# The gated convolution's input projection with its three column blocks walked innermost, in two sets of three PSUM banks

## The chip, the cores and the metric

One core of a Trainium2 chip runs the whole program. The metric is the device time of one execution in microseconds (us), the median over several runs. PSUM is the accumulator memory that TensorE writes; it has eight banks here, and one matmul writes into one bank.

## The reference, cut to what matters

The program is one inference step of a small decoder: a gated short convolution layer, shared keys and values, one forgetting-attention layer, and a gated feed after each of the two layers. It runs on 1024 prompt tokens and 64 sample tokens, 1088 columns in all. The change lies in the convolution layer, in the product `h @ w_in`:

```python
def short_conv_layer(x, conv_state, g, w_in, conv_w, w_out):
    h = rmsnorm(x, g)
    b_gate, c_gate, xin, z = jnp.split(h @ w_in, 4, axis=-1)
    u = c_gate * xin
    u_pad = jnp.concatenate([conv_state.astype(u.dtype), u], axis=1)
    T = u.shape[1]
    conv = conv_w[0] * u_pad[:, 0:T]
    for j in range(1, CONV_W):
        conv = conv + conv_w[j] * u_pad[:, j:j + T]
    y = b_gate * conv * jax.nn.silu(z)
    return x + y @ w_out, u_pad[:, -(CONV_W - 1):]
```

`h` has 1024 features, `w_in` is 1024 x 4096, everything is float32.

## The kernel before

Activations lie transposed: 128 features on the partitions, the 1088 tokens along the free axis, eight such chunks k = 0 to 7 (`KC`). The tokens are cut into three column blocks (`BLK`): 364, 364 and 360 columns. An fp32 product is made of three cheaper ones: each operand is split into a rounded part and a rest (`w_hi` and `w_lo`, `Hhi` and `Hlo`), and `w_hi*Hhi`, `w_hi*Hlo` and `w_lo*Hhi` are added up in PSUM (lines 560, 561, 562). An output tile is 128 output features by 1088 tokens: 3 blocks x 8 chunks x 3 products = 72 matmuls, each with a weight load of its own.

The input projection is 32 such tiles: a loop over j = 0 to 7, and in it t = 0 to 3 for the four parts of `w_in` (c_gate, xin, z, b_gate in that order). Line 615 calls `tile(...)` with bank 0, so that every tile writes banks 0, 1 and 2, one for each column block. `tile` has two orders:

- With `hr` given (t = 0 here) chunk k is the outer loop, since at the start of the stage the chunks of h arrive one by one: for each k it makes three products of block 0, three of block 1, three of block 2. The bank changes after each three products.
- Without `hr` (t = 1, 2, 3) the block is the outer loop: all 24 products of block 0, then those of block 1, then those of block 2. The bank changes after 24 products.

Before the first product of a block, `free(b)` makes TensorE wait until the bank's last content has been taken out; the last product of a block raises the semaphore `block_done`. What takes a tile out of PSUM differs: t = 0 is copied to scrA by ScalarE (line 984), t = 1 is multiplied with scrA into scrU by VectorE (lines 1293 and 1295), t = 2 goes through ScalarE's silu into scrZ (line 986), t = 3 is multiplied with scrC into Y by VectorE (line 1319). These raise `act_evac` (ScalarE) and `dve_evac` (VectorE), three per tile.

Beside that, the same engines prepare weights. The weight buffers are doubled (`par`): SyncE loads tile n's weights, GpSimd multiplies in the norm's gain (line 490), ScalarE makes `w_hi` (line 937) as soon as tile n - 2 is done with the buffer, VectorE makes `w_lo` (line 1232), and that releases TensorE (`w_split`). Each engine's queue is in order: on VectorE `w_lo` of tile j, t = 3 stands behind the convolution of t = 1 (lines 1299 to 1311), and on ScalarE `w_hi` for the next tile stands behind the three evacuations of t = 0 or t = 2.

After the 32 tiles comes the output projection, whose operand Y is split in two by ScalarE and VectorE (lines 967 and 1261); it may begin when all of Y is written. Its tiles, and those of the feed, go through the same `tile` function with `hr` given for every other tile.

Of the kernel before, what the change touches and what calls it, by code (L numbers as in the profile page):

```python
# [20 lines left out]
ALU = mybir.AluOpType  # L21
# [45 lines left out]
for _kb in range(8):  # L67
# [11 lines left out]
    "tensor": {"block_done": 6, "score": 1, "turned": 1, "pv": 1, "s_score": 2, "s_pv": 1},  # L79
    "vector": {"n0_acc": 2, "n1_acc": 2, "n2_acc": 2, "w_split": 2, "x_sum": 2, "dve_evac": 6, "o_free": 1, "o_done": 1,  # L80
               "p_lo": 1, "s_kt1": 1, "s_pt1": 1, "s_osb": 1, "s_out": 1},
    "scalar": {"exp": 1, "s_kt0": 1, "s_exp": 1, "s_pt0": 1},
    "sync": {"kv_out": 16, "y_out": 16},
}
START = {name: n for per in LEAD.values() for name, n in per.items()}
# [7 lines left out]
def program(nc, a, o, d):  # L93

    es = ExitStack()
    with es:
# [451 lines left out]
        def _(pe):  # L548
            for k, n in LEAD["tensor"].items():
                pe.sem_inc(sems[k], n)  # L550
            mm, tp = pe.matmul, pe.transpose

            def tile(n, par, bank, free, hr=None, k0=0, nk=KC, hi=Hhi, lo=Hlo):

                pe.wait_ge(sems["w_split"], START["w_split"] + n + 1)
                def products(b, k):
                    s, e = BLK[b]
                    out = PS[:, bank + b, 0:e - s]
                    wh, wl = whi[:, par, k0 + k, :], wlo[:, par, k0 + k, :]
                    mm(out, wh, hi[:, k, s:e], start=(k == 0), stop=False)  # L560
                    mm(out, wh, lo[:, k, s:e], start=False, stop=False)  # L561
                    last = mm(out, wl, hi[:, k, s:e], start=False, stop=(k == nk - 1))  # L562
                    if k == nk - 1:
                        last.then_inc(sems["block_done"], 1)
                if hr is not None:
                    for k in range(nk):
                        pe.wait_ge(sems["h_ready"], hr + k + 1)
                        for b in range(NB):
                            if k == 0:
                                free(b)  # L570
                            products(b, k)
                else:
                    for b in range(NB):
                        free(b)
                        for k in range(nk):
                            products(b, k)
# [33 lines left out]
            with pe.Fori(0, KC) as j:  # L610
                for t in range(4):

                    free = [lambda b: pe.wait_ge(sems["dve_evac"], START["dve_evac"] + 6 * j - 3 + b + 1), lambda b: pe.wait_ge(sems["act_evac"], 6 * j + b + 1),
                            lambda b: pe.wait_ge(sems["dve_evac"], START["dve_evac"] + 6 * j + b + 1), lambda b: pe.wait_ge(sems["act_evac"], 6 * j + 3 + b + 1)][t]
                    tile(4 * j + t, t % 2, 0, free, hr=0 if t == 0 else None)

            def out_tiles(n0, ed0, hr):
                with pe.Fori(0, KC // 2) as i:
# [4 lines left out]
            def feed(r, n0, ea0, ed0, hr):  # L623

                pe.wait_ge(sems[f"ple{r}_in"], 48)
                for c in range(PC):
                    for h_, src in enumerate((sA, sZ, sU)):
                        if c:
                            pe.wait_ge(sems[f"ple{r}_lo"], h_ + 1)
                        if h_ < 2:  # L630
                            for i in range(4):
                                last = tp(PS[:, 3 + h_, i * P:(i + 1) * P], src[:, i * PLE + c * P:i * PLE + (c + 1) * P], ident[:, :])
                        else:
                            last = tp(PS[:, 5, 0:NS], src[0:NS, c * P:(c + 1) * P], ident[0:NS, 0:NS])
                        last.then_inc(sems[f"ple{r}_turned"], 1)
                pe.wait_ge(sems[f"ple{r}_lo"], 6)
                pe.wait_ge(sems["dve_evac"], START["dve_evac"] + ed0)
                with pe.Fori(0, KC // 2) as i:
                    for u in range(2):
                        n, par = n0 + 2 * i + u, (n0 + u) % 2  # L640
                        tile(n, par, 0, lambda b: pe.wait_ge(sems["act_evac"], ea0 + 6 * i + 3 * u - 3 + b + 1), hr=hr if u == 0 else None)
                        tile(n, par, 3, lambda b: pe.wait_ge(sems["dve_evac"], START["dve_evac"] + ed0 + 6 * i + 3 * u - 3 + b + 1),
                             k0=KC, nk=PC, hi=PTh, lo=PTl)

# [5 lines left out]
            feed(0, N_A3, EA_A3, ED_A3, 16)  # L650
            norm_sum(1)

            pe.wait_ge(sems["act_evac"], EA_F)
            tile(N_F, N_F % 2, 0, lambda b: None, hr=24)

            pe.wait_ge(sems["s_logf"], 16 * DB * PAGES)
# [15 lines left out]
            def dense_piece(j, half, p):  # L672

                i, b, k = 2 * half + p // 24, p % 24 // KC, p % KC
                g_ = 4 * j + 3 + i
                par = (N_B1 + 3 + i) % 2
                if p % 24 == 0:
                    pe.wait_ge(sems["w_split"], START["w_split"] + N_B1 + g_ + 1)
                if k == 0:
                    pe.wait_ge(sems["act_evac"], EA_B1 + 3 * g_ - 3 + b + 1)  # L680
                s, e = BLK[b]
                out = PS[:, b, 0:e - s]
                wh, wl = whi[:, par, k, :], wlo[:, par, k, :]
                mm(out, wh, Hhi[:, k, s:e], start=(k == 0), stop=False)  # L684
                mm(out, wh, Hlo[:, k, s:e], start=False, stop=False)  # L685
                last = mm(out, wl, Hhi[:, k, s:e], start=False, stop=(k == KC - 1))  # L686
                if k == KC - 1:
                    last.then_inc(sems["block_done"], 1)
# [87 lines left out]
            half_pair(NPAIR - 1, 1, False)  # L776


            pe.wait_ge(sems["act_evac"], EA_B2)
            pe.wait_ge(sems["exp"], START["exp"] + 16 * NPAIR)  # L780
            pe.wait_ge(sems["p_lo"], START["p_lo"] + 24 * NPAIR)
            pe.wait_ge(sems["o_done"], START["o_done"] + 4 * NPAIR)
# [121 lines left out]
            out_tiles(N_B2, ED_B2, 32)  # L904
            feed(1, N_B3, EA_B3, ED_B3, 40)
            pe.wait_ge(sems["dve_evac"], START["dve_evac"] + ED_END)
            pe.wait_ge(sems["act_evac"], EA_END)
            pe.wait_ge(sems["n2_acc"], START["n2_acc"] + KC)
            for tt in range(9):
                n = P if tt < 8 else NS  # L910
# [313 lines left out]
        def _(ve):  # L1224
# [56 lines left out]
            def conv_layer(j, last):  # L1281
                for t in range(4):
# [4 lines left out]
                    ve.drain()  # L1287
                    if t == 1:
                        for b, (s, e) in enumerate(BLK):
                            ve.wait_ge(sems["act_evac"], 6 * j + b + 1)  # L1290
                            ve.wait_ge(sems["block_done"], START["block_done"] + 12 * j + 3 + b + 1)
                            m = min(e, SEQ)
                            ins = tt_(Up[:, 2 + s:2 + m], PS[:, b, 0:m - s], sA[:, s:m], ALU.mult)
                            if e > SEQ:
                                ins = tt_(Us[:, :, 2:], PS[:, b, SEQ - s:e - s].rearrange("p (b t) -> p b t", b=DB),
                                          sA[:, SEQ:e].rearrange("p (b t) -> p b t", b=DB), ALU.mult)
                            ins.then_inc(sems["dve_evac"], 1)
                        g = lambda r, n=1: GT[:, bass.ds(j, 1), r:r + n].rearrange("p a n -> p (a n)")
                        ve.tensor_copy(Us[:, :, 0:2], g(G_ST, 16).rearrange("p (b w) -> p b w", b=DB))
                        ve.drain()  # L1300
                        cs = sC[:, SEQ:].rearrange("p (b t) -> p b t", b=DB)
                        for w in range(CW):
                            for dst, src in ((sC[:, 0:SEQ], Up[:, w:w + SEQ]), (cs, Us[:, :, w:w + DS])):
                                if w == 0:
                                    ts_(dst, src, g(G_CW), None, ALU.mult)
                                else:
                                    stt(out=dst, in0=src, scalar=g(G_CW + w), in1=dst, op0=ALU.mult, op1=ALU.add)
                            ve.drain()
                        ucj = at_pair(uc, j).rearrange("p a n -> p (a n)")
                        ve.tensor_copy(ucj[:, 0:2], Up[:, SEQ:SEQ + 2])  # L1310
                        ve.tensor_copy(ucj[:, 2:18].rearrange("p (b w) -> p b w", b=DB), Us[:, :, DS:])
                    if t == 2:
                        ve.wait_ge(sems["act_evac"], 6 * j + 6)
                        tt_(sC[:, :], sC[:, :], sZ[:, :], ALU.mult)
                        ve.drain()
                    if t == 3:
                        for b, (s, e) in enumerate(BLK):
                            ve.wait_ge(sems["block_done"], START["block_done"] + 12 * j + 9 + b + 1)
                            tt_(at_pair(Y, j).rearrange("p a n -> p (a n)")[:, s:e], PS[:, b, 0:e - s], sC[:, s:e],
                                ALU.mult).then_inc(sems["dve_evac"], 1)  # L1320
            peeled(ve, KC, conv_layer)

# [20 lines left out]
            def feed(r, n0, b0, ea0, h0):  # L1343
# [10 lines left out]
                def body(i, last):  # L1354
                    for u in range(2):
# [4 lines left out]
                        else:  # L1360
                            w_lo(n % 2, n + 2 * i, nk=KC + PC)
                        for b, (s, e) in enumerate(BLK):
                            ve.wait_ge(sems["act_evac"], ea0 + 6 * i + 3 * u + b + 1)
                            ve.wait_ge(sems["block_done"], START["block_done"] + b0 + 12 * i + 6 * u + 3 + b + 1)
                            tt_(sg[:, u, s:e], sg[:, u, s:e], PS[:, 3 + b, 0:e - s], ALU.mult).then_inc(sems["dve_evac"], 1)
                        ve.drain()
# [291 lines left out]
```

## Time and profile before

| | us |
|---|---|
| median of 3 runs (lowest, highest) | 1946.63 (1946.03, 1947.12) |
| profiled execution, first to last instruction (its span) | 1943.1 |
| TensorE busy with matmuls | 1765.1 |
| VectorE busy | 885.6 |
| ScalarE busy | 721.3 |
| GpSimd busy | 265.3 |

The profiled execution has no other time of its own than its span; the median of the runs is 3.5 us more, which is what lies around the first and last instruction. A matmul's recorded duration includes its way through the array and is a model; two matmuls in a row overlap in the rows. What a matmul costs in a stream is the distance from its start to the next one's start. Starts are printed to 0.01 us. The granted clock of TensorE is printed as a share of full speed; 1.00 is 2.4 GHz and 0.50 is 1.2 GHz.

### The profile page before, as it was taken

How to read it: one execution, taken by the hardware profiler on the slowest of the kernel's cores; microseconds unless marked ns; L12 is line 12 of the kernel's file. 1: busy time of each engine (PE TensorE's matmuls, PEld its weight loads, DVE VectorE, ACT ScalarE, POOL GpSimd, SP SyncE). 2: the span in 40 equal slices, each digit the busy share in tenths (PEclk: the TensorE clock that was granted, in tenths of full speed). 3: DMA queues.
4: the chain of work that ended last, by engine and by line, in shares of the span. 5: the costliest groups of instructions: out<-in, count | busy, mean ns of one | idle time of the engine just before them, and what ended most of it. 6: DMA issues, size and time to landing. Idle time of an engine off the chain costs nothing.

```text
span 1943.1 us, 33338 instructions
## 1 busy us (share of the span) xinstructions
PE 1765.1 (91%) x11871; PEld 1611.6 (83%) x11871; DVE 885.6 (46%) x1379; ACT 721.3 (37%) x1174; POOL 265.3 (14%) x229
## 2 busy tenths in 40 slices
PE   3699999999999958999999999999779999899997
PEld 2699999999989948888888888888656666699997
DVE  5722222224253374555555556555544444523543
ACT  3311211112043233565656555565533233401432
POOL 1311111110000021222222122222110000000010
PEclk7999999999999979999999999999869999899998
DMA  3011111111211023211101021110318778721102
GB/s 127 23 45 45 47 50 47 45 44 44 72 41 42 8 97 92 57 46 34 56 23 59 19 78 45 34 56 23 132 51 307 265 269 327 276 86 57 41 27 92
DMA packets 163424, 161.57 MB, mean 83 GB/s; under 512 B 18188, under 2 KB 140172, under 8 KB 163126
## 3 DMA queue, kind: packets, MB, share of 16 engines
q1 hardware_dynamic: 163382, 161.03, 24.9%
q8 instruction: 24, 0.39, 0.1%
q14 instruction: 18, 0.15, 0.0%
HBM read 137.20 MB, written 23.80 MB: 83 GB/s over the span
## 4 chain that ended last, share of the span: by engine, by line
PE 73%; DVE 10%; ACT 6%; issue 5%; DVEq 3%; ACTq 2%; POOL 1%; DMA 0%; SPq 0%; POOLq 0%
PE PS L560 14%; PE PS L562 14%; PE PS L561 14%; PE PS L684 4%; PE PS L686 3%; PE PS L685 3%; PE PS L743 3%; PE PS L790 3%; PE PS L731 2%; DVE small L1410 2%; PE PS L857 2%; PE PS L714 2%; PE PS L812 2%; DVE pTl L1421 1%; DVE Hlo L1261 1%
## 5 line engine op out<-in xcount | busy, mean ns | idle before, releaser
L560 PE MATMUL PS<-Hhi,w_hi 128*128 128x364 f32 (+1 forms) x1560 | 519.3, 333 | 58.7 <-DVE Hlo L1261 57.6
L562 PE MATMUL PS<-Hhi,w_lo 128*128 128x364 f32 (+1 forms) x1560 | 515.8, 331 | 0.0
L561 PE MATMUL PS<-Hlo,w_hi 128*128 128x364 f32 (+1 forms) x1560 | 513.4, 329 | 0.0
L560 PEld LDWEIGHTS PS<-Hhi,w_hi 128*128 128x128 f32 x1560 | 297.2, 190 | 66.2 <-issue 44.2
L561 PEld LDWEIGHTS PS<-Hlo,w_hi 128*128 128x128 f32 x1560 | 296.6, 190 | 0.0
L562 PEld LDWEIGHTS PS<-Hhi,w_lo 128*128 128x128 f32 x1560 | 296.1, 190 | 0.0
L684 PE MATMUL PS<-Hhi,w_hi 128*128 128x364 f32 (+1 forms) x768 | 274.0, 357 | 0.1
L686 PE MATMUL PS<-Hhi,w_lo 128*128 128x364 f32 (+1 forms) x768 | 252.4, 329 | 0.0
L685 PE MATMUL PS<-Hlo,w_hi 128*128 128x364 f32 (+1 forms) x768 | 251.8, 328 | 0.0
L490 POOL TENSOR_TENSOR w_raw<-w_raw,GT 128x1024 f32<-128x1024 f32 x65 | 128.6, 1980 | 692.8 <-DMA w_raw<-in_w_kv 383.2
L937 ACT ACTIVATE w_hi<-w_raw 128x1024 fp32r<-128x1024 f32 (+1 forms) x97 | 105.8, 1091 | 293.4 <-PE PS L562 289.4
L1232 DVE TENSOR_TENSOR w_lo<-w_raw,w_hi 128x1024 fp32r<-128x1024 f32 (+1 forms) x97 | 126.0, 1299 | 140.2 <-ACT w_hi L937 136.7
L1421 DVE TENSOR_TENSOR pTl<-PS,pTh 128x512 fp32r<-128x512 f32 x192 | 103.5, 554 | 122.6 <-ACT pTh L1067 120.2
L1059 ACT ACTIVATE Pb<-PS,small 128x128 f32<-128x128 f32 (+7 forms) x128 | 94.8, 740 | 160.8 <-DVE small L1410 160.8
L684 PEld LDWEIGHTS PS<-Hhi,w_hi 128*128 128x128 f32 x768 | 146.8, 191 | 0.7 <-DVE w_lo L1232 0.2
L519 POOL TENSOR_SCALAR Pb<-Pb,small 128x128 f32<-128x128 f32 (+7 forms) x128 | 95.1, 747 | 378.1 <-DVE small L1415 378.1
L685 PEld LDWEIGHTS PS<-Hlo,w_hi 128*128 128x128 f32 x768 | 145.9, 190 | 0.0
L686 PEld LDWEIGHTS PS<-Hhi,w_lo 128*128 128x128 f32 x768 | 144.7, 188 | 0.0
L1067 ACT ACTIVATE pTh<-PS 128x512 fp32r<-128x512 f32 x192 | 89.7, 487 | 96.9 <-PE PS L731 93.6
L1410 DVE TENSOR_REDUCE small<-PS 128x1 f32<-128x128 f32 (+7 forms) x128 | 95.6, 748 | 37.2 <-PE PS L717 36.9
L743 PE MATMUL PS<-pTh,VS 128*128 128x512 f32 x192 | 73.5, 383 | 35.1 <-DVE pTl L1421 35.0
L731 PE MATMUL PS<-ident,Pb 128*128 128x128 f32 x576 | 94.5, 285 | 6.7 <-POOL Pb L519 6.7
(230 smaller groups left out, 2286.3 us busy)
## 6 DMA issues: line engine op xcount, KB each, us to landing
Kpages<-in_cache_k SPq DMA_DIRECT2D x64, 512.0 KB, 5.7
Vpages<-in_cache_v SPq DMA_DIRECT2D x64, 512.0 KB, 5.5
w_raw<-in_w_in_a SPq DMA_DIRECT2D x64, 256.0 KB, 3.0
w_raw<-in_w_ple_gate SPq DMA_DIRECT2D x16, 512.0 KB, 3.7
w_raw<-in_w_kv SPq DMA_DIRECT2D x32, 256.0 KB, 3.1
w_raw<-in_w_in_b SPq DMA_DIRECT2D x32, 256.0 KB, 3.0
parked_x<-X SPq DMA_DIRECT2D x8, 544.0 KB, 5.0
X<-parked_x SPq DMA_DIRECT2D x8, 544.0 KB, 7.7
```

Source lines behind the costliest of these rows:

```text
L490: g.tensor_tensor(w, w, GT[:, :, r:r + 1].to_broadcast([P, KC, P]), ALU.mult).then_inc(sems["w_gained"], 1)
L560: mm(out, wh, hi[:, k, s:e], start=(k == 0), stop=False)
L561: mm(out, wh, lo[:, k, s:e], start=False, stop=False)
L562: last = mm(out, wl, hi[:, k, s:e], start=False, stop=(k == nk - 1))
L684: mm(out, wh, Hhi[:, k, s:e], start=(k == 0), stop=False)
L685: mm(out, wh, Hlo[:, k, s:e], start=False, stop=False)
L686: last = mm(out, wl, Hhi[:, k, s:e], start=False, stop=(k == KC - 1))
L731: last = tp(PS[:, 5 + kb % 2, qi * P:(qi + 1) * P], Pb[:, off:off + P], ident[:, :])
L743: last = mm(PS[:, 7, q0 * P:512], VS[:, kb, hh, :], x[:, kb % 2, q0 * P:512], start=(kb == 0 and x is pTh), stop=(kb == nkb - 1 and x is pTl))
L1232: tt_(wlo[:, par, 0:nk, :], raw[:, par, 0:nk, :], f(whi[:, par, 0:nk, :]), ALU.subtract).then_inc(sems["w_split"], 1)
L1410: ve.reduce_max(small[:, qb:qb + 1], score_bank(qb)[:, 0:n], AXX, negate=True).then_inc(sems["rowmax"], 1)
L1421: tt_(pTl[:, kb % 2, q0 * P:512], PS[:, 5 + kb % 2, q0 * P:512], f(pTh[:, kb % 2, q0 * P:512]), ALU.subtract).then_inc(sems["p_lo"], 1)
```

## The change

A new function `across` replaces `tile` for the 32 tiles of the input projection. Chunk k stays or becomes the outer loop, in it come the three products, and the three column blocks are innermost. So the first product of a chunk is made for blocks 0, 1 and 2, then the second, then the third, and each matmul writes another bank than the one before. The three sums of a tile are open at the same time and all end with the tile's last three matmuls. Tiles alternate between banks 0 to 2 (t = 0 and 2) and banks 3 to 5 (t = 1 and 3); before a tile's first product one wait asks for the last block of the tile two before it to be taken out. To make that wait hold in the first round, `act_evac` starts at 6, and every wait on it adds that offset.

```diff
-    "scalar": {"exp": 1, "s_kt0": 1, "s_exp": 1, "s_pt0": 1},
+    "scalar": {"act_evac": 6, "exp": 1, "s_kt0": 1, "s_exp": 1, "s_pt0": 1},
...
+            def across(n, par, bank, free, hr=None):
+
+                pe.wait_ge(sems["w_split"], START["w_split"] + n + 1)
+                free(NB - 1)
+                for k in range(KC):
+                    if hr is not None:
+                        pe.wait_ge(sems["h_ready"], hr + k + 1)
+                    wh, wl = whi[:, par, k, :], wlo[:, par, k, :]
+                    for x, (w, h) in enumerate(((wh, Hhi), (wh, Hlo), (wl, Hhi))):
+                        for b, (s, e) in enumerate(BLK):
+                            last = mm(PS[:, bank + b, 0:e - s], w, h[:, k, s:e], start=(k == 0 and x == 0), stop=(k == KC - 1 and x == 2))
+                            if k == KC - 1 and x == 2:
+                                last.then_inc(sems["block_done"], 1)
...
-                    free = [lambda b: pe.wait_ge(sems["dve_evac"], START["dve_evac"] + 6 * j - 3 + b + 1), lambda b: pe.wait_ge(sems["act_evac"], 6 * j + b + 1),
-                            lambda b: pe.wait_ge(sems["dve_evac"], START["dve_evac"] + 6 * j + b + 1), lambda b: pe.wait_ge(sems["act_evac"], 6 * j + 3 + b + 1)][t]
-                    tile(4 * j + t, t % 2, 0, free, hr=0 if t == 0 else None)
+                    free = [lambda b: pe.wait_ge(sems["act_evac"], START["act_evac"] + 6 * j - 3 + b + 1), lambda b: pe.wait_ge(sems["dve_evac"], START["dve_evac"] + 6 * j - 3 + b + 1),
+                            lambda b: pe.wait_ge(sems["act_evac"], START["act_evac"] + 6 * j + b + 1), lambda b: pe.wait_ge(sems["dve_evac"], START["dve_evac"] + 6 * j + b + 1)][t]
+                    across(4 * j + t, t % 2, 3 * (t % 2), free, hr=0 if t == 0 else None)
...
-                            ins = tt_(Up[:, 2 + s:2 + m], PS[:, b, 0:m - s], sA[:, s:m], ALU.mult)
+                            ins = tt_(Up[:, 2 + s:2 + m], PS[:, 3 + b, 0:m - s], sA[:, s:m], ALU.mult)
...
-                            tt_(at_pair(Y, j).rearrange("p a n -> p (a n)")[:, s:e], PS[:, b, 0:e - s], sC[:, s:e],
+                            tt_(at_pair(Y, j).rearrange("p a n -> p (a n)")[:, s:e], PS[:, 3 + b, 0:e - s], sC[:, s:e],
```

The rest of the diff adds `START["act_evac"]` to the other waits on `act_evac`.

## Rows read from the trace of the kernel before

**Rows 1.** The page's head: the span, and the busy time of each engine.

```profile
span 1943.1 us, 33338 instructions
...
PE 1765.1 (91%) x11871; PEld 1611.6 (83%) x11871; DVE 885.6 (46%) x1379; ACT 721.3 (37%) x1174; POOL 265.3 (14%) x229
```

**Rows 2.** Busy time by window, tiles 2 to 31: window, length, each engine's busy, PEclk, DMA.

```profile
90.81:448.90 358.09, 358.08 (x2162) 357.53 (x2160) 105.53 (x163) 69.81 (x88) 51.78 (x27) 1.00 0.16 45
```

**Rows 3.** Timeline of TensorE (start, duration): first products of tiles and blocks.

```profile
78.80 0.43 PE L560 MATMUL PS<-Hhi,w_hi 128*128 128x364 f32 x1 [1.19 <-DVE w_lo L1232]
...
162.43 0.33 PE L560 MATMUL PS<-Hhi,w_hi 128*128 128x364 f32 x1
...
174.29 0.33 PE L560 MATMUL PS<-Hhi,w_hi 128*128 128x364 f32 x1
...
178.29 0.33 PE L560 MATMUL PS<-Hhi,w_hi 128*128 128x364 f32 x1
...
182.25 0.32 PE L560 MATMUL PS<-Hhi,w_hi 128*128 128x360 f32 x1
...
186.24 0.33 PE L560 MATMUL PS<-Hhi,w_hi 128*128 128x364 f32 x1
```

**Rows 4.** Timeline of TensorE, one chunk of a t = 0 tile: bank changes.

```profile
122.13 0.33 PE L560 MATMUL PS<-Hhi,w_hi 128*128 128x364 f32 x1
...
122.46 0.33 PE L562 MATMUL PS<-Hhi,w_lo 128*128 128x364 f32 x1
122.63 0.33 PE L560 MATMUL PS<-Hhi,w_hi 128*128 128x364 f32 x1
...
122.96 0.33 PE L562 MATMUL PS<-Hhi,w_lo 128*128 128x364 f32 x1
123.12 0.33 PE L560 MATMUL PS<-Hhi,w_hi 128*128 128x360 f32 x1
...
123.45 0.32 PE L562 MATMUL PS<-Hhi,w_lo 128*128 128x360 f32 x1
123.61 0.33 PE L560 MATMUL PS<-Hhi,w_hi 128*128 128x364 f32 x1
```

**Rows 5.** Feed after the output projection, at half clock: two timeline rows, one window.

```profile
557.23 0.50 PE L560 MATMUL PS<-Hhi,w_hi 128*128 128x360 f32 x1
...
558.13 0.51 PE L560 MATMUL PS<-Hhi,w_hi 128*128 128x364 f32 x1
...
555.20:559.70 4.50, 4.45 (x15) 4.46 (x16) 4.50 (x4) 4.50 (x6) 0.00 (x0) 0.50 0.00 0
```

**Rows 6.** Timeline of VectorE after tile t = 1: last evacuation, next two weight splits.

```profile
138.72 0.47 DVE L1293 TENSOR_TENSOR scrU<-PS,scrA 128x296 f32<-128x296 f32 x1 [3.45 <-PE PS L562]
...
144.20 1.23 DVE L1232 TENSOR_TENSOR w_lo<-w_raw,w_hi 128x1024 fp32r<-128x1024 f32 x1
...
152.67 1.23 DVE L1232 TENSOR_TENSOR w_lo<-w_raw,w_hi 128x1024 fp32r<-128x1024 f32 x1
```

**Rows 7.** Timeline of ScalarE: evacuation of a t = 0 tile, and a weight split.

```profile
125.79 1.45 ACT L984 ACTIVATE scrA<-PS 128x364 f32<-128x364 f32 x3 [9.80 <-PE PS L562]
...
151.35 1.07 ACT L937 ACTIVATE w_hi<-w_raw 128x1024 fp32r<-128x1024 f32 x1 [0.20 <-issue]
```

**Rows 8.** Timeline, all engines: the end of the stage.

```profile
448.93 0.53 DVE L1319 TENSOR_TENSOR Y<-PS,scrC 128x360 f32<-128x360 f32 x1 [3.45 <-PE PS L562]
449.49 4.12 ACT L967 ACTIVATE Hhi<-Y 128x1088 fp32r<-128x1088 f32 x4 [10.85 <-DVE Y L1319]
...
452.17 0.43 PE L560 MATMUL PS<-Hhi,w_hi 128*128 128x364 f32 x1 [3.28 <-DVE Hlo L1261]
```

**Rows 9.** Windows after idle TensorE: the clock behind two such gaps.

```profile
452.20:464.00 11.80, 11.80 (x72) 11.77 (x72) 9.84 (x10) 6.36 (x7) 0.00 (x0) 1.00 0.10 27
...
1675.80:1679.20 3.40, 0.07 (x1) 0.07 (x2) 2.88 (x5) 1.54 (x5) 0.00 (x0) 1.00 1.03 414
1679.30:1682.70 3.40, 3.40 (x17) 3.16 (x17) 0.97 (x3) 2.55 (x6) 0.00 (x0) 0.50 0.65 266
```

More of the change, by code:

```diff
@@ L640, in feed @@
                         n, par = n0 + 2 * i + u, (n0 + u) % 2
-                        tile(n, par, 0, lambda b: pe.wait_ge(sems["act_evac"], ea0 + 6 * i + 3 * u - 3 + b + 1), hr=hr if u == 0 else None)
+                        tile(n, par, 0, lambda b: pe.wait_ge(sems["act_evac"], START["act_evac"] + ea0 + 6 * i + 3 * u - 3 + b + 1), hr=hr if u == 0 else None)
                         tile(n, par, 3, lambda b: pe.wait_ge(sems["dve_evac"], START["dve_evac"] + ed0 + 6 * i + 3 * u - 3 + b + 1),
@@ L651, in _ @@
             norm_sum(1)
-            pe.wait_ge(sems["act_evac"], EA_F)
+            pe.wait_ge(sems["act_evac"], START["act_evac"] + EA_F)
             tile(N_F, N_F % 2, 0, lambda b: None, hr=24)
@@ L679, in dense_piece @@
                 if k == 0:
-                    pe.wait_ge(sems["act_evac"], EA_B1 + 3 * g_ - 3 + b + 1)
+                    pe.wait_ge(sems["act_evac"], START["act_evac"] + EA_B1 + 3 * g_ - 3 + b + 1)
                 s, e = BLK[b]
@@ L776, in _ @@
             half_pair(NPAIR - 1, 1, False)
-            pe.wait_ge(sems["act_evac"], EA_B2)
+            pe.wait_ge(sems["act_evac"], START["act_evac"] + EA_B2)
             pe.wait_ge(sems["exp"], START["exp"] + 16 * NPAIR)
@@ L906, in _ @@
             pe.wait_ge(sems["dve_evac"], START["dve_evac"] + ED_END)
-            pe.wait_ge(sems["act_evac"], EA_END)
+            pe.wait_ge(sems["act_evac"], START["act_evac"] + EA_END)
             pe.wait_ge(sems["n2_acc"], START["n2_acc"] + KC)
@@ L1289, in conv_layer @@
                         for b, (s, e) in enumerate(BLK):
-                            ve.wait_ge(sems["act_evac"], 6 * j + b + 1)
+                            ve.wait_ge(sems["act_evac"], START["act_evac"] + 6 * j + b + 1)
                             ve.wait_ge(sems["block_done"], START["block_done"] + 12 * j + 3 + b + 1)
                             m = min(e, SEQ)
-                            ins = tt_(Up[:, 2 + s:2 + m], PS[:, b, 0:m - s], sA[:, s:m], ALU.mult)
+                            ins = tt_(Up[:, 2 + s:2 + m], PS[:, 3 + b, 0:m - s], sA[:, s:m], ALU.mult)
                             if e > SEQ:
-                                ins = tt_(Us[:, :, 2:], PS[:, b, SEQ - s:e - s].rearrange("p (b t) -> p b t", b=DB),
+                                ins = tt_(Us[:, :, 2:], PS[:, 3 + b, SEQ - s:e - s].rearrange("p (b t) -> p b t", b=DB),
                                           sA[:, SEQ:e].rearrange("p (b t) -> p b t", b=DB), ALU.mult)
@@ L1312, in conv_layer @@
                     if t == 2:
-                        ve.wait_ge(sems["act_evac"], 6 * j + 6)
+                        ve.wait_ge(sems["act_evac"], START["act_evac"] + 6 * j + 6)
                         tt_(sC[:, :], sC[:, :], sZ[:, :], ALU.mult)
@@ L1362, in body @@
                         for b, (s, e) in enumerate(BLK):
-                            ve.wait_ge(sems["act_evac"], ea0 + 6 * i + 3 * u + b + 1)
+                            ve.wait_ge(sems["act_evac"], START["act_evac"] + ea0 + 6 * i + 3 * u + b + 1)
                             ve.wait_ge(sems["block_done"], START["block_done"] + b0 + 12 * i + 6 * u + 3 + b + 1)
```

## The prediction, made before the change was run

> **What bounds the kernel now.** I read the page's head first: of a span of 1943.1 us TensorE is busy 91%, VectorE 46%, ScalarE 37% [rows 1]. The span is 3.5 us under the median of the runs, 1946.63; I take those 3.5 us as fixed and make the sum against 1946.63. Then the windows over the stage that changes: from the start of tile 2 to the end of tile 31 TensorE is busy for 358.08 of 358.09 us, at the full clock, while VectorE has work for 105.53 and ScalarE for 69.81 us [rows 2]. So nothing waits in this stage; only a shorter distance between products, or a new wait, can move its time.
>
> Then the timeline of TensorE, for that distance. A t = 0 tile, bank changing after three products, lasts 174.29 - 162.43 = 11.86 us; the t = 1 tile behind it, bank changing after 24, 186.24 - 174.29 = 11.95 us [rows 3]. That is 11.86/72 = 164.7 ns and 11.95/72 = 166.0 ns a product. Over the stage (8 tiles of the first kind, 24 of the second) the mean is 165.7 ns for 2304 products. This pair is a small trial of the change that the trace already holds: same data and same number of products, other order.
>
> What is in those 166 ns? In the half-clock window behind the stage three products of 360 columns take 558.13 - 557.23 = 0.90 us, 300 ns each [rows 5], which is 360 columns at 1.2 GHz and nothing else. At 2.4 GHz the mean of 362.7 columns would then be 151.1 ns; the stage has 14.6 ns more. A cost of writing the same bank again, if it were counted in TensorE's own cycles, would show at half clock as well, where the three products also share a bank. It doesn't.
>
> **The change part by part.**
>
> Order of products in t = 1, 2, 3. The number of products and of weight loads stays. Now the bank changes with every product; the trace has no row for that. Nearest is the t = 0 tile. In one of its chunks the step is 123.61 - 122.13 = 1.48 us for nine products (164.4 ns), and the distances across a change of bank read 0.17 (bank 0 to 1), 0.16 (1 to 2) and 0.16 (2 to 0) [rows 4]. In the block-wise tile the first block takes 4.00 us for 24 products, the second 3.96, the third 3.99 although its products are four columns shorter [rows 3]: the distance follows the pattern of lengths and starts more than the bank. I take the t = 0 tile's value for all tiles: 24 x (11.86 - 11.95) = -2.2 us. Both bounds come from the printed starts, which show 0.16 or 0.17: at 160 ns 2304 x -5.7 = -13.1 us, at 170 ns 2304 x 4.3 = +9.9 us. The value is nearer the middle because each of the three changes of bank that the new order repeats stands in rows 4, and 0.49 us over three is 163 ns, with up to 0.01 us of rounding in each.
>
> Order in t = 0: it changes only from three in a row to one; at the same value it costs nothing. In tile 0 each chunk still waits for h, in the same order.
>
> Evacuations. Until now a block-wise tile's first two blocks were taken out beside its own products; now all three end together and are taken out beside the next tile. With t = 0 that is so already: three copies, 1.45 us in all from 125.79, around that tile's end at 162.43 - 3 x 11.95 = 126.58, and no gap on TensorE [rows 2, 3, 7]. For t = 1, VectorE's two earlier multiplies move behind the tile's end, some 2 x 0.5 us. Behind them stand the convolution and `w_lo` for t = 3, which now ends at 144.20 + 1.23 = 145.43 us [rows 6]; at 146.4 it would still be about 4 us ahead of tile t = 3, which begins one tile length before the next t = 0 tile, at 162.43 - 11.95 = 150.48 [rows 3]. For t = 2, two silu evacuations (0.5 us each, as the copies) move behind the tile's end, ahead of `w_hi` at 151.35 and `w_lo` at 152.67 [rows 6, 7]; 1 us later than 153.9 is still over 7 us ahead of 162.43. The PSUM waits ask for the tile two before, a whole tile (11.9 us) back, and its evacuation ends 2 us after it. So these moves cost nothing, covered by the next tile's products; without that cover each would add up to 1 us a tile, 32 us in all. The wait of tile 1 for its first weights, 1.19 us [rows 3], is set by weight preparation ahead of any evacuation and stays.
>
> The Trainium skill speaks against the change here: its page Perfetto Trace Analysis (Optimizing Tensor Performance, Matmuls) wants independent groups to rotate through banks so that one group's evacuation runs beside the next one's products. By that rule, read strictly for the three groups of a tile, those 32 us would be lost; by rows 3 and 7 the second set of banks keeps the cover, except in the last tile.
>
> The last tile has no cover. Its last multiply began at 448.93, the split of Y followed at 449.49 and TensorE began again at 452.17 [rows 8]. Now three multiplies begin about two products earlier (448.6) and take some 0.5 us each, so Y is whole at about 450.1 instead of 449.46: +0.7 us. Weight prefetch is not late: its DMAs and gains wait for the weight splits, which move by under 1 us.
>
> Offsets: one semaphore increment at ScalarE's start, long before its first work, and two PSUM waits fewer per tile. Nothing, as no gap stands at a tile's start now [rows 2].
>
> Clock at that gap. TensorE idles 3.28 us there now, and the clock stays at 1.00 afterwards [rows 8, 9]; elsewhere 3.40 us of near idleness were followed by 3.40 us at 0.50 [rows 9]. With 4 us idle a drop is possible. It would cost half of its length, so 1.7 us for 3.4 and 3.4 us for twice that. I leave it out of the sum (the gap stays short) and put it in the range.
>
> Sum: -2.2 + 0.7 = -1.5 us, 1945.1 us. A measurement of this kernel can tell 0.2%, 3.9 us, from no change; so this counts as no change.
>
> **The rivals.**
>
> The gain grows with the changes of bank. A t = 0 tile has 24 changes, the others 3; 0.09 us over 21 is 4.3 ns each. With 72 in every tile: 24 x 69 x 4.3 ns = 7.1 us and 8 x 48 x 4.3 ns = 1.7 us, so -8.8 + 0.7: 1938.5 us. For it: the t = 0 tile is the shorter one [rows 3]. Against it: the distances across a change [rows 4] are not shorter than those within a bank as a whole.
>
> Same-bank accumulation is the whole excess. 2304 x 14.6 ns = 33.6 us, so 1913.7 us. Rows 4 and 5 speak against it. The Trainium skill's page TensorE: Matmul & The Clock Gate (Back-to-back issue gap) gives columns/2.4 GHz + 2.5 ns for a lone stream, 153.6 ns here, an estimate by which about 28 us could be won; the same section says that with weight loads both set the spacing, and the trace has a load for each product and 165.7 ns, so it bears out the second statement.
>
> The order lands in the long pattern (slower). Place: every product of the 32 tiles. Its price is that of the change from bank 0 to bank 1, 0.17 us [rows 4]; if all three changes took that, 2304 x 4.3 = +9.9, with the +0.7 at the end 1957.2 us. It decides from 165.7 + (3.9 - 0.7)/2304 = 167.1 ns a product. Against it: the other two changes read 0.16.
>
> Nothing changes in the products: each tile keeps its distance and only the end is paid, 1947.3 us. That is also the case in which the order isn't what sets the 14.6 ns at all.
>
> **How the numbers follow.** Forecast 1945.1 us: 0.46. Gain by bank change: 0.26. Whole excess: 0.04. Long pattern: 0.12. Nothing in the products: 0.12. So faster 0.30, same 0.46 + 0.12 = 0.58, slower 0.12. The forecast's own range is 1943 to 1948.5 (with a clock drop of 3.4 us). The range leaves out the whole excess and the long pattern and goes from 1937.0, just under the gain by bank change, to 1949.5, the case of nothing in the products with most of a clock drop.
>
> **What would show it.** Right: tiles of about 11.86 us for every t, TensorE without gaps from tile 2 to 31, the three last multiplies in a row and TensorE back 0.7 us later after them. A step of nine products at 1.44 us or less would be the gain by bank change, at 1.51 or more the long pattern. Wrong altogether: an idle row ahead of a tile's first product, named by `w_lo`, scrA or scrZ, or fewer weight loads than products.

## The result: slower by 0.16%, and the profile after

| | before | changed |
|---|---|---|
| median of 15 runs each (us) | 1946.63 | 1950.62 |
| lowest, highest | 1945.05, 1951.39 | 1945.21, 1952.16 |
| span of the profiled execution | 1943.1 | 1948.5 |

The ratio of the changed kernel to the one before is 1.0016, 95% interval 1.0009 to 1.0024, so 1.8 to 4.7 us are lost. A second comparison gave 1.0018 (1.0009 to 1.0028). The forecast was 1945.1 us, with a range up to 1949.5. Four executions in the comparisons of this study took over 500 us longer than the others of their kernel, and the ratios and the spreads below leave them out. The changed kernel's profiled execution took 1950.32 us, 1.8 us more than its span of 1948.5. All 15 executions lie 1.7 to 1.8 us above their own spans, so only about half of the 3.5 us that I had read as lying around the span does so; the rest would be the spread between executions.

The head of the page after, beside [rows 1]: the same number of matmuls, and TensorE busy for 6.1 us more, where the span is 5.4 us longer. So the longer span is time in which TensorE works, not time in which it waits.

```profile
span 1948.5 us, 33291 instructions
...
PE 1771.2 (91%) x11871; PEld 1616.8 (83%) x11871; DVE 882.6 (45%) x1379; ACT 718.2 (37%) x1174; POOL 265.2 (14%) x229
```

The window of [rows 2] again, in the changed kernel. No new wait: TensorE is busy throughout, but in the same time it makes 2151 products instead of 2162. (The counts in brackets take in products that reach into the window.)

```profile
90.81:448.90 358.09, 358.09 (x2151) 358.09 (x2150) 102.37 (x163) 66.56 (x88) 51.73 (x27) 1.00 0.16 45
```

Timeline of TensorE in the changed kernel, the answer to [rows 3, 4]. The first three rows are first products of three tiles in a row (t = 0, 1, 2); the other three stand for three products each, one in each bank.

```profile
163.50 0.33 PE L563 MATMUL PS<-Hhi,w_hi 128*128 128x364 f32 x1
...
175.50 0.33 PE L563 MATMUL PS<-Hhi,w_hi 128*128 128x364 f32 x1
...
187.50 0.33 PE L563 MATMUL PS<-Hhi,w_hi 128*128 128x364 f32 x1
...
450.00 0.66 PE L563 MATMUL PS<-Hhi,w_hi 128*128 128x364 f32 x3
450.50 0.66 PE L563 MATMUL PS<-Hlo,w_hi 128*128 128x364 f32 x3
451.00 0.66 PE L563 MATMUL PS<-Hhi,w_lo 128*128 128x364 f32 x3
```

From tile 2 on every tile takes 12.00 us, where it was 11.86 or 11.95. The step is 0.50 us for three products, 166.7 ns each, and it stays that regular to the last tile. (Tile 0 waits for the chunks of h; tile 1, which starts after the wait for its weights, takes 12.09 us.) The end of the stage, all engines, and the clock behind it, beside [rows 8, 9]:

```profile
451.36 1.42 DVE L1333 TENSOR_TENSOR Y<-PS,scrC 128x364 f32<-128x364 f32 x3 [8.11 <-PE PS L563]
452.81 1.11 ACT L981 ACTIVATE Hhi<-Y 128x1088 fp32r<-128x1088 f32 x1 [10.99 <-DVE Y L1333]
...
455.49 0.67 PE L574 MATMUL PS<-Hhi,w_hi 128*128 128x364 f32 x1 [3.83 <-DVE Hlo L1275]
...
455.40:458.90 3.50, 3.41 (x11) 3.42 (x12) 3.50 (x4) 3.50 (x5) 0.00 (x0) 0.51 0.00 0
```

The three multiplies now stand in one row, all behind the tile's end, and TensorE's gap is 3.83 us instead of 3.28. Behind it the clock is at half speed for 3.4 us, which it wasn't before.

Against the profile before, the differences of matching products give the account. The first product of tile 1 comes 0.60 us later (78.80 to 79.40); it waits for its weights there as before, and two profiles of the unchanged kernel differ at that point by 0.56 us, so I don't count this to the change. The last product of the stage is 2.77 us later, so the products cost 2.17. The first output tile begins 3.32 us later: the gap costs 0.55. The second output tile begins 4.88 us later: the half clock costs 1.56. After that the difference stays between 4.86 and 5.06 us up to the last matmul.

### The profile page after: what moved, and what is told of

It reads as the page before. It is cut to its first block, busy times and chain, and to the rows that moved or that the text cites. A ratio compares the mean times of both kernels' runs of the same rounds, so it can differ in the third digit from the quotient of the medians.

```text
span 1948.5 us, 33291 instructions
## 1 busy us (share of the span) xinstructions
PE 1771.2 (91%) x11871; PEld 1616.8 (83%) x11871; DVE 882.6 (45%) x1379; ACT 718.2 (37%) x1174; POOL 265.2 (14%) x229
## 4 chain that ended last, share of the span: by engine, by line
PE 72%; DVE 10%; ACT 6%; issue 5%; DVEq 3%; ACTq 2%; DMA 1%; POOL 1%; SPq 0%; POOLq 0%
PE PS L563 19%; PE PS L574 8%; PE PS L576 7%; PE PS L575 7%; PE PS L698 4%; PE PS L700 3%; PE PS L699 3%; PE PS L757 3%; PE PS L804 3%; PE PS L745 2%; DVE small L1424 2%; PE PS L871 2%; PE PS L728 2%; PE PS L826 2%; DVE pTl L1435 1%
## 5 line engine op out<-in xcount | busy, mean ns | idle before, releaser
L574 PE MATMUL PS<-Hhi,w_hi 128*128 128x364 f32 (+1 forms) x792 | 266.3, 336 | 36.0 <-DVE Hlo L1275 36.0
L698 PE MATMUL PS<-Hhi,w_hi 128*128 128x364 f32 (+1 forms) x768 | 274.0, 357 | 0.1
L576 PE MATMUL PS<-Hhi,w_lo 128*128 128x364 f32 (+1 forms) x792 | 263.0, 332 | 0.0
L575 PE MATMUL PS<-Hlo,w_hi 128*128 128x364 f32 (+1 forms) x792 | 262.6, 332 | 0.0
L700 PE MATMUL PS<-Hhi,w_lo 128*128 128x364 f32 (+1 forms) x768 | 252.4, 329 | 0.0
L699 PE MATMUL PS<-Hlo,w_hi 128*128 128x364 f32 (+1 forms) x768 | 251.9, 328 | 0.0
L563 PE MATMUL PS<-Hhi,w_hi 128*128 128x364 f32 (+1 forms) x768 | 171.3, 331 | 22.7 <-DVE Hlo L1275 21.6
L574 PEld LDWEIGHTS PS<-Hhi,w_hi 128*128 128x128 f32 x792 | 152.5, 193 | 40.1 <-issue 29.7
L563 PE MATMUL PS<-Hlo,w_hi 128*128 128x364 f32 (+1 forms) x768 | 170.5, 330 | 0.0
L563 PE MATMUL PS<-Hhi,w_lo 128*128 128x364 f32 (+1 forms) x768 | 170.1, 330 | 0.0
L563 PEld LDWEIGHTS PS<-Hhi,w_hi 128*128 128x128 f32 x768 | 133.7, 189 | 25.8 <-issue 15.0
L575 PEld LDWEIGHTS PS<-Hlo,w_hi 128*128 128x128 f32 x792 | 152.5, 192 | 0.0
L576 PEld LDWEIGHTS PS<-Hhi,w_lo 128*128 128x128 f32 x792 | 152.0, 192 | 0.0
L698 PEld LDWEIGHTS PS<-Hhi,w_hi 128*128 128x128 f32 x768 | 146.8, 191 | 0.7 <-DVE w_lo L1246 0.2
L699 PEld LDWEIGHTS PS<-Hlo,w_hi 128*128 128x128 f32 x768 | 145.9, 190 | 0.0
L700 PEld LDWEIGHTS PS<-Hhi,w_lo 128*128 128x128 f32 x768 | 144.7, 188 | 0.0
```

The costliest lines, as they stand in the source:

```text
L563: last = mm(PS[:, bank + b, 0:e - s], w, h[:, k, s:e], start=(k == 0 and x == 0), stop=(k == KC - 1 and x == 2))
```

## The experiments

Three things had to be told apart: whether the 12.00 us come from the changes of bank or from the order of operands (which weights and columns follow each other); whether the value belongs to the order at all or can fall either way; and whether the fall of the clock belongs to the longer gap.

**Chunk order in all tiles, two bank sets.** The bank changes at every third product.

```diff
-                    for x, (w, h) in enumerate(((wh, Hhi), (wh, Hlo), (wl, Hhi))):
-                        for b, (s, e) in enumerate(BLK):
+                    for b, (s, e) in enumerate(BLK):
+                        for x, (w, h) in enumerate(((wh, Hhi), (wh, Hlo), (wl, Hhi))):
```

> The changed kernel, but inside a chunk three products of block 0, then three of block 1, then three of block 2 (the bank changes every third product), for all 32 tiles; two bank sets and evacuation at the tile's end stay. Theory A (the distance between products is set by the order of operands, lengths and starts, not by the bank): every tile takes 11.84 to 11.87 us, against 12.00 in the changed kernel and 11.95 in three quarters of the tiles before; the stage is about 2.2 us shorter than before and 4.5 us shorter than in the changed kernel; the gap behind the stage is between 3.3 and 3.8 us. Median 1944 to 1946 us. Theory B (fewer changes of bank are better, since the change with 72 per tile got longer): the tiles lie between 11.95 (3 changes) and 12.00 (72 changes), about 11.97.

Measured: median 1945.08 us, ratio to before 0.9982 (0.9973 to 0.9991). First products of two tiles in a row in its timeline:

```profile
161.68 0.33 PE L563 MATMUL PS<-Hhi,w_hi 128*128 128x364 f32 x1
...
173.52 0.33 PE L563 MATMUL PS<-Hhi,w_hi 128*128 128x364 f32 x1
```

11.84 us for every tile from tile 2 on, the value of theory A and outside that of theory B. Bank sets and evacuations are those of the changed kernel here, so neither of them makes the 12.00 us; the order of the nine products in a chunk does. All 11 executions lie between 1942.43 and 1946.25 us, while 13 of the changed kernel's 15 took 1949.66 us or more. The kernel is faster than before though its clock, too, fell behind the stage, with a gap no longer than before.

**One bank, and banks that rotate.** These two put the changed kernel's order on one bank, and the old order on changing banks. In both, a tile is taken out after its last product; the edits to the evacuations are left out here.

```diff
-                            last = mm(PS[:, bank + b, 0:e - s], w, h[:, k, s:e], start=(k == 0 and x == 0), stop=(k == KC - 1 and x == 2))
+                            last = mm(PS[:, bank, 0:e - s], w, h[:, k, s:e], start=(k == 0 and x == 0 and b == 0), stop=(k == KC - 1 and x == 2 and b == 2))
...
```

> The changed kernel's order of operands to the letter, but all three blocks of a tile are added up in one bank, so the bank never changes within a tile; each tile is taken out after its last product. Its sums leave the three blocks unseparated. Theory A (order of operands): tiles stay at 12.00 us. Theory B (change of bank costs 0.65 ns per product): tiles go back to 11.95 us or under. Theory C (writing the same bank again costs something that the other patterns hide): tiles become longer than 12.00 us, by up to 14 ns per product, 13 us per tile.

```diff
+                m = 0
+                for b, (s, e) in enumerate(BLK):
+                    for k in range(KC):
...
+                            last = mm(PS[:, bank + m % 3, 0:e - s], w, h[:, k, s:e], start=(m < 3), stop=(m >= 69))
+                            m += 1
...
```

> The order of operands of the kernel before (all 24 products of a block, then the next block) in all tiles, but product m writes bank m modulo 3, so the bank changes with every product as in the changed kernel. Its sums are spread over three banks instead of one per block. Theory A (order of operands): tiles of 11.95 us with blocks of 4.00, 3.96 and 3.99 us, as before. Theory B (change of bank): tiles of 12.00 us. Theory C: shorter than 11.95.

Measured, first the kernel with rotating banks and the old order (first products of three tiles in a row):

```profile
169.96 0.33 PE L564 MATMUL PS<-Hhi,w_hi 128*128 128x364 f32 x1
...
181.91 0.33 PE L564 MATMUL PS<-Hhi,w_hi 128*128 128x364 f32 x1
...
193.87 0.33 PE L564 MATMUL PS<-Hhi,w_hi 128*128 128x364 f32 x1
```

11.95 us, with the bank changing at every product: as before, as theory A has it. (Its first tile, block by block too, waits longer for h; its total of 1958.18 us isn't compared.) The other kernel, one bank and the changed order, showed 11.84 us per tile and 1945.75 us. That fits neither theory A (12.00) nor C (longer; its 14 ns a product would be 1 us a tile, not 13); it would fit B, but B wants 12.00 us of the rotating banks, which showed 11.95. So I ran it again with many executions, beside the changed kernel and the kernel before.

> The kernel with the changed kernel's order of operands and one bank per tile once more, now with many executions; its sums leave the three blocks unseparated. Open is whether its 11.84 us per tile belongs to it, or is one of two spacings (1.480 or 1.500 us for nine products) into which the stream of the changed kernel's order may settle in any execution. Theory D (each order and bank pattern has its own spacing): tiles of 11.84 us again, executions in one group about 5 us under those of the changed kernel, near the kernel before. Theory E (drawn anew in each execution, whatever the banks): two groups 5 us apart, some at the level of the changed kernel, and perhaps tiles of 12.00 us in the profile.

> The changed kernel as it is, for another look. Theory D: tiles of 12.00 us again. Theory E: 12.00 or 11.84. In both, the gap behind the stage is 3.8 us; whether the clock falls in it is seen here a second time (it fell in the first profile, and at gaps of 3.4 to 3.6 us in two of the experiments).

Timeline of the one-bank kernel, first run; each row is three products:

```profile
441.08 0.66 PE L563 MATMUL PS<-Hhi,w_hi 128*128 128x364 f32 x3
441.58 0.66 PE L563 MATMUL PS<-Hlo,w_hi 128*128 128x364 f32 x3
442.07 0.66 PE L563 MATMUL PS<-Hhi,w_lo 128*128 128x364 f32 x3
442.56 0.49 PE L563 MATMUL PS<-Hhi,w_hi 128*128 128x364 f32 x2
```

And the same kernel, second run:

```profile
440.38 0.66 PE L563 MATMUL PS<-Hhi,w_hi 128*128 128x364 f32 x3
440.88 0.66 PE L563 MATMUL PS<-Hlo,w_hi 128*128 128x364 f32 x3
441.38 0.66 PE L563 MATMUL PS<-Hhi,w_lo 128*128 128x364 f32 x3
441.88 0.66 PE L563 MATMUL PS<-Hhi,w_hi 128*128 128x364 f32 x3
```

1.48 us for nine products in one run, 1.50 in the other: the same instructions, two spacings, each held through the whole stage. The second run's median is 1951.7 us (1948.73 to 1954.27), ratio 1.0020 (1.0011 to 1.0029), no better than the changed kernel. So with one bank the stage can be as slow as with three, and the bank is not the cause; what differs between the two runs of this kernel is how the stream settled, as theory E has it. Of the two groups of executions that theory E also expected, this run shows one: all eleven lie at the level of the changed kernel, and the first run's single execution stays the only short one. The changed kernel again settled at 12.00 us per tile, median 1950.94:

```profile
162.62 0.33 PE L563 MATMUL PS<-Hhi,w_hi 128*128 128x364 f32 x1
...
174.62 0.33 PE L563 MATMUL PS<-Hhi,w_hi 128*128 128x364 f32 x1
```

In the first comparison two of its 15 executions took 1945.21 and 1945.60 us, about 5 us under the others; 31 tiles x 0.16 us would be 5.0 us. That these two had settled in the short spacing is likely but not shown, since they have no profile.

**Does the stream keep the spacing in which it arrives?** Here the t = 0 tiles have the chunk order, t = 1, 2, 3 the changed one.

```diff
+                    order = [(x, b) for b in range(NB) for x in range(3)] if hr is not None else [(x, b) for x in range(3) for b in range(NB)]
...
```

> The changed kernel, but its t = 0 tiles have the chunk order (three products of a block in a row), t = 1, 2, 3 keep the blocks innermost. Each execution now enters the new order eight times instead of once. If the stream keeps the spacing in which it arrives (the 1.480 us per nine products of the chunk order), all tiles take 11.84 us and the stage is 5 us shorter than in the changed kernel. If it settles anew at each entry, the tiles t = 1 to 3 take 11.84 us in some rounds and 12.00 us in others. If the blocks-innermost order draws the stream to 1.500 us each time, they take 12.00 us in all rounds, with the step inside the first chunks of t = 1.

First products of a t = 0 tile, its three followers, and the next t = 0 tile:

```profile
162.51 0.33 PE L566 MATMUL PS<-Hhi,w_hi 128*128 128x364 f32 x1
...
174.35 0.33 PE L566 MATMUL PS<-Hhi,w_hi 128*128 128x364 f32 x1
...
186.34 0.33 PE L566 MATMUL PS<-Hhi,w_hi 128*128 128x364 f32 x1
...
198.34 0.33 PE L566 MATMUL PS<-Hhi,w_hi 128*128 128x364 f32 x1
...
210.34 0.33 PE L566 MATMUL PS<-Hhi,w_hi 128*128 128x364 f32 x1
```

11.84, then 11.99, 12.00, 12.00, and so in every round from the second on. In this profile the order with blocks 0, 1, 2 innermost draws the stream to the long spacing early in the first tile of the three (it is only 0.01 us short of 12.00), even when it arrives in the short one (1950.02 us, one execution).

**Another sequence of blocks.** Innermost 0, 2, 1 instead of 0, 1, 2.

```diff
-                        for b, (s, e) in enumerate(BLK):
+                        for b, (s, e) in ((0, BLK[0]), (2, BLK[2]), (1, BLK[1])):
...
```

> The changed kernel with the innermost order of blocks 0, 2, 1 (364, 360, 364 columns) instead of 0, 1, 2; each tile is taken out after its last product. Banks change with every product as before. If the long spacing of 500 ns per three products belongs to any blocks-innermost order, tiles take 12.00 us (or 11.84 in an execution that settles in the short one). If it belongs to the sequence of starts and lengths, another value appears, between 11.7 and 12.1 us.

> The kernel with the innermost order of blocks 0, 2, 1 once more, with many executions, to see whether its 11.84 us per tile was a draw. If the sequence 0, 2, 1 belongs to the short spacing: 11.84 us per tile again and executions in one group near the kernel before (short products, longer gap behind the stage), ratio 0.999. If it is drawn as in the one-bank kernel: 12.00 us per tile in the profile or a second group of executions 5 us above the first.

First products of two tiles in a row, first run (a row here holds two products, the first of them counts):

```profile
161.67 0.49 PE L563 MATMUL PS<-Hhi,w_hi 128*128 128x364 f32 x2
...
173.51 0.49 PE L563 MATMUL PS<-Hhi,w_hi 128*128 128x364 f32 x2
```

And in the second run (three products to a row):

```profile
161.50 0.66 PE L563 MATMUL PS<-Hhi,w_hi 128*128 128x364 f32 x3
...
173.34 0.66 PE L563 MATMUL PS<-Hhi,w_hi 128*128 128x364 f32 x3
```

11.84 us in both profiles. The executions of the second run lie between 1944.38 and 1952.54 us, ratio 1.0001 (0.9989 to 1.0013); the kernel before spread as widely beside it (1944.45 to 1952.74), so whether each execution had the short spacing can't be told. Bank changes are as many as in the changed kernel, so their number doesn't make the long spacing. That the sequence does is likely and not shown: two short profiles of this sequence stand against five long ones and one short one of the sequence 0, 1, 2, and the one-bank kernel shows that a single profile can fall either way.

**The gap and the clock.** The changed kernel with its last tile block by block, and the kernel before once more.

```diff
+                    if last and t == 3:
+                        tile(4 * j + t, t % 2, 3 * (t % 2), free)
+                    else:
+                        across(4 * j + t, t % 2, 3 * (t % 2), free, hr=0 if t == 0 else None)
...
```

> The changed kernel, but its last tile (j = 7, t = 3) is made block by block, so that two of its three evacuations lie beside its own products again. Theory: the gap on TensorE behind the stage falls from 3.83 to about 3.3 us, the clock stays at 1.00 through the first output tile, which takes 11.9 instead of 13.5 us; together 2.1 us less than the changed kernel's profile, so a median near 1948.5 us. Rival: the clock falls with the shorter gap too (or fell in the profile by chance), then only 0.5 us is won.

> The kernel before as it is, for another look. If the fall of the clock behind the stage belongs to the longer gap, the clock stays at 1.00 again and the first output tile takes 11.9 us. If it is a matter of where the gap falls in time, it may fall here too, with the gap of 3.28 us unchanged, and the first output tile takes 13.4 to 13.5 us. Tiles 11.95 us with t = 0 tiles at 11.85 in either case.

The kernel with the covered last tile: last product of the stage, first output product, a window behind it.

```profile
450.34 0.33 PE L576 MATMUL PS<-Hhi,w_lo 128*128 128x360 f32 x1
453.94 0.43 PE L574 MATMUL PS<-Hhi,w_hi 128*128 128x364 f32 x1 [3.27 <-DVE Hlo L1279]
...
454.90:458.20 3.30, 3.30 (x12) 3.30 (x12) 3.30 (x4) 3.30 (x4) 0.00 (x0) 0.50 0.00 0
```

The kernel before, second profile, the same three rows:

```profile
448.01 0.33 PE L562 MATMUL PS<-Hhi,w_lo 128*128 128x360 f32 x1
451.62 0.43 PE L560 MATMUL PS<-Hhi,w_hi 128*128 128x364 f32 x1 [3.28 <-DVE Hlo L1261]
...
452.10:455.40 3.30, 3.30 (x13) 3.30 (x12) 3.30 (x4) 3.30 (x4) 0.00 (x0) 0.50 0.00 0
```

The gap came back to 3.27 us as expected, but the clock fell all the same, and it falls in the unchanged kernel's second profile after the very gap of 3.28 us that it had survived in the first [rows 8, 9]. So my theory, that the longer gap brought the fall, isn't borne out; the 1.56 us in the account above are no sure part of the change. The first profile of the kernel before was the odd one: in every other profile of this study the clock fell there, for 3.4 or 6.8 us, at gaps from 3.27 us up. What spared the first stays open. (The gaps of 3.4 to 3.6 us in my expectation for the changed kernel's second profile are 3.27 and 3.28 us when read as idle time.)

The covered last tile gave a median of 1947.86 us, ratio 0.9997 (0.9988 to 1.0006). The profile shows the gap's 0.55 us won back and the tiles still at 12.00 us. By these rows it should be some 2 us slower than the kernel before, while the interval of the ratio ends at 1.2 us. So the median came out near the expected 1948.5 us, but not by the clock that I had expected it from. Its executions spread from 1945.01 to 1950.67 us; whether some of them ran in the short spacing is open, since only one has a profile.

**What beats both.** The chunk as outer loop in every tile of the kernel, first with the old single bank set, then with two sets in the input projection. The second kernel joins this edit to that of the first experiment.

```diff
-                if hr is not None:
-                    for k in range(nk):
-                        pe.wait_ge(sems["h_ready"], hr + k + 1)
-                        for b in range(NB):
-                            if k == 0:
-                                free(b)
-                            products(b, k)
-                else:
-                    for b in range(NB):
-                        free(b)
-                        for k in range(nk):
-                            products(b, k)
+                for k in range(nk):
+                    if hr is not None:
+                        pe.wait_ge(sems["h_ready"], hr + k + 1)
+                    for b in range(NB):
+                        if k == 0:
+                            free(b)
+                        products(b, k)
```

> The kernel before with the chunk as outer loop in every tile (input projection, output projections, feeds and the small tile ahead of the attention), one bank set as before. Theory: every tile of 72 products takes 11.84 us: 24 tiles of the input projection and 16 of output and feed win 0.11 us each, 4.4 us, the small feed tiles perhaps 0.5 us more; the evacuation of the first two blocks begins 1 and 0.5 us ahead of the tile's end, so that the single bank set makes TensorE wait little or not at all. Median about 1942 us, ratio to the kernel before 0.9975. Rival: the single bank set lets TensorE wait for the third block's evacuation, up to 0.7 us a tile, and the kernel is slower than before.

> The chunk order in every tile, as in the run with one bank set, and two bank sets in the input projection. In that run some tiles took up to 11.893 us, with distances of up to 191 ns at their first products, where a bank's evacuation was still under way. With two sets all tiles of the input projection take 11.84 us: 0.6 us less than with one set in all. Median about 1941 us, ratio to the kernel before 0.996 to 0.997.

First products of a t = 0, t = 1 and t = 2 tile with one bank set:

```profile
209.43 0.35 PE L560 MATMUL PS<-Hhi,w_hi 128*128 128x364 f32 x1
...
221.32 0.33 PE L560 MATMUL PS<-Hhi,w_hi 128*128 128x364 f32 x1
...
233.16 0.33 PE L560 MATMUL PS<-Hhi,w_hi 128*128 128x364 f32 x1
```

With two sets:

```profile
209.19 0.33 PE L563 MATMUL PS<-Hhi,w_hi 128*128 128x364 f32 x1
...
221.03 0.33 PE L563 MATMUL PS<-Hhi,w_hi 128*128 128x364 f32 x1
...
232.87 0.33 PE L563 MATMUL PS<-Hhi,w_hi 128*128 128x364 f32 x1
```

One set: 1941.37 us, ratio 0.9968 (0.9956 to 0.9979). Two sets: 1943.04 us, ratio 0.9975 (0.9964 to 0.9985). The first came out as expected, the second 2 us above the expected 1941. The second set saves the 0.02 to 0.05 us that a t = 0 tile pays with one set (11.86 or 11.89 against 11.84; the rows show one of 11.89), but in the totals the two can't be told apart. Both beat the kernel before and the changed one; the simpler of the two, with one loop order and the old banks, has the lowest median measured here.

## Why the prediction was wrong

The step that failed is "I take the t = 0 tile's value for all tiles: 24 x (11.86 - 11.95) = -2.2 us". In its place the runs showed +2.2 us: tiles of 12.00 us for every t, also the t = 0 tiles, for which I had written that the change of order costs nothing. I had written myself that the distance follows the pattern of lengths and starts more than the bank; then I put the three distances across a change of bank together (0.49 us for three) as if each pair of neighbours had a price of its own. It hasn't: with the same changes of bank in another sequence three products took 0.50 us, and with the old sequence on changing banks nothing moved (11.95 us). In this stream the distance goes with the sequence that repeats, and with which of two steady spacings the stream settles in; why it settles in one or the other stays open. The neighbours in rows 4 came from the sequence with the short one. As bounds my own figures held: the long spacing, 166.7 ns, lies between 160 and 170 ns, and the block of 4.00 us in [rows 3] had it already. That row, 24 products at 166.7 ns, was the better guide to the upper end than the t = 0 tile was to the middle.

Point by point:

- No new wait in the stage: right [rows 2, and the window after]. The evacuations moved behind the tiles' ends without a gap on TensorE; with the second bank set they ran beside the next tile's products, except in the last tile.
- The end of the stage, +0.7 us: right in kind, measured 0.55.
- The clock: I left its fall out of the sum and priced it at 1.7 us for 3.4 us; measured 1.56 for 3.41. But it comes with the old gap as well.
- The gain by changes of bank (0.26) and the whole excess (0.04): refuted, for the new order with a change at every product got longer, the old order with a change at every product stays at 11.95 us, and the new order in one bank takes no longer than in three (12.00, once 11.84). The argument that a same-bank cost would have shown at half clock [rows 5] fits this, and I should have let it take more from the first of these two. What sets the 14.6 ns above 151.1, the weight loads among others, no run separated.
- The long pattern (0.12) is the rival that came nearest: the products got longer, but to 166.7 ns, not to 170, and the step of 1.50 us for nine stayed just under the mark of 1.51 that I had set for it. Products and end, +2.2 and +0.55 us, are 2.7, inside the measured 1.8 to 4.7 us; what makes the medians differ by 4.0 isn't known in full. The range fell short since its upper end was the case of nothing in the products plus most of a clock fall, and left this rival out.

## What to carry to other kernels

When TensorE never waits, an order of products is worth what its steady spacing is, and that can't be put together from single distances of another order: measure the whole repeating sequence, in more than one execution. Rotating the banks bought nothing for the products here; what the second bank set served was the evacuations. Where one tile of a kernel already runs in a shorter order, copy that order as it is.

## What was not expected of the hardware

- The same products with the same weight loads ran at 164.4 ns (1.480 us for nine) or 166.7 ns (0.500 us for three), and once settled held it for the rest of the stage, over 350 us. The one-bank kernel showed the one value in one profile and the other in the next. At half clock neither excess is there [rows 5]. What decides between them stays open. The banks don't. The sequence of blocks went with it so far (0, 1, 2 innermost: long in five profiles of six; 0, 2, 1: short in both), too few to be sure; the chunk order (three products of a block in a row) was short in every profile that has it.
- The clock fell to half behind the same 3.28 us gap in one profile of the unchanged kernel and not in another; one profile of a clock is no rule.
